# FF2 of a two-block transformer in fp32: activation sums, weight splits and outputs in another order, the norm row copied to SBUF, a longer held product

## Chip, cores and metric

One core of a Trainium2 chip. The metric is the device time of one execution in microseconds; lower is better.

## The reference

Two transformer blocks run one after the other on x of 1024 tokens by 1024 columns, in float32. The part that matters here is the feed-forward end of the second block:

```python
h = rmsnorm(x, pre_ffn_w[l])
f = (jax.nn.silu(h @ w_gate[l]) * (h @ w_up[l])) @ w_down[l]
x = x + rmsnorm(f, post_ffn_w[l])
```

`w_gate` and `w_up` are 1024 by 2816, `w_down` is 2816 by 1024. Everything before it (attention, convolution, pooling, the first feed-forward part, differential and neighbourhood attention) is computed by the same program ahead of this part, and no edit touches it.

## The kernel before, in words

**Precision.** Every fp32 product is made of three fp32r matmuls, high x high, high x low, low x high. A weight or an activation is split in two steps: ACT copies `raw` to fp32r (the high half), DVE subtracts it from `raw` (the low half). So a weight goes SP (load), ACT (high), DVE (low), TensorE. Activations lie transposed: features on 128 partitions, tokens along the free dimension, in two halves of 512 tokens (`HALF`).

**Engines.** There is no scheduler. For each engine a method writes its instructions in order (`pe_ff2`, `act_ff2`, `dve_ff2`, `pool_ff2`, `sp_ff2`), and semaphores join them. An engine works strictly down its list: a wait holds all that stands behind it. SP issues all DMAs of this part.

**The start of FF2 (in the trace from about 2174 us).** The 22 feature tiles of gate and up are each `g` and `u`. The first three (`PLAIN`) are plain products. `pe_ff2` runs g1's second half with the norm's statistics `stats7` inside it, u1 with the norm's rows `rows7` inside, then g2 and u2. On DVE: `gate_half` and `gate_whole` multiply the gate product by the norm row (RB), `gated` multiplies `up` by the Silu, `norm_recip` is the reciprocal of the norm, `w_low` makes a weight's low half. On ACT: `w_high` makes the high half, `up` and `up_whole` copy the up product to UU (`up_whole` waits until the spill of an earlier tile has read it), `silu`, `norm_sqrt`, the copy of the norm row to RB.

**Strassen.** The other 19 tiles (`NQ`) run by Strassen's scheme in seven parts a tile (`part`), each 12 matmuls of 512 columns. It needs sums of activation blocks: `second(k)` on ACT makes a scaled copy (`snap`), `sums(k)` on DVE makes four sums into `tr`, `sums_high(k)` on ACT and `sums_low(k)` on DVE split them into `th` and `tl`. Four k in all. SP's first weight loads of this stage (`gate_load(0)`, `up_load(0)`, into `swr`) wait for the last sums. The weights get sums (`s_sums`, on `swr`) and splits (`swh`, `swl`) of their own. The results of a tile go through `gate`, `shared`, `shared_end`, `gate_end`, `value`, `value_end` on DVE. `spill(i)` on SP writes each finished tile of 128 x 1024 (`uu`) to HBM (`scr_u`).

**The down product.** 88 slabs w = 22 p + k: token half p // 2, output half p % 2 (four output tiles n, each in a bank of its own), 22 slabs of features k. A slab is a weight tile of 128 x 512 (`dwr`, split into `dwt`; nine buffers, so that slab w's load waits for the end of slab w - 9) and an activation tile of 128 x 512 read back from `scr_u` (`DUR`, split into `DU`, in the trace `AH`, `AL` and `du`), and 12 matmuls of 512 columns. p = 0 and 2 use banks 0 to 3, p = 1 and 3 banks 4 to 7. `evacuate(p)` on DVE multiplies four finished banks by RB into YD. ACT squares them (`square`), POOL adds the squares (`accD`), TensorE turns these into the norm of the first token half: `stats(8, ...)` into bank 7, `rows(0, 6)` into bank 6. DVE then scales the eight output tiles of that half by the row in bank 6 (eight `scalar_tensor_tensor`, counted in `fmu`), and POOL adds x.

**The held part and the end.** Of the last p only the first `HELD` slabs are run over 512 tokens; ACT copies these partial sums to YD. The remaining 22 - `HELD` slabs are run for 256 tokens and then for the other 256, so that the final norm can begin with the first 256. The loop over w waits for all 88 slabs' low halves before these two groups. `out(g, n)` on DVE adds the partial sum and multiplies by RB.

**The turn.** In the last Strassen tile (n = 18) DVE makes seven weight splits and four activation splits between `gate_end` and `value`.

The wait of TensorE at slab 66 (`pe_ff2`), and the splits ahead of `value` at the turn (`dve_ff2`):

```python
            if w == 66:
                q.wait_ge(S.fmu, 8)
...
                for w in range(7):
                    d_low(w)
                    if w < 4:
                        u_low(w)
            value(n)
```

In the trace all matmuls have line 225, DVE's `tensor_tensor` line 193, its `scalar_tensor_tensor` line 196, ACT's activations line 190, DMA issues line 232.

## Time and profile before

| | |
|---|---|
| median of 3 runs | 2907.8 us (2907.36 to 2908.87) |
| the profiled execution | 2905.17 us, span 2902.9 us |
| TensorE busy | 2820.1 us (97%), 12895 matmuls |
| DVE, ACT, POOL busy | 1563.9 us (54%), 1032.5 us (36%), 369.5 us (13%) |
| mean granted TensorE clock | 0.99 |

The profiled execution's own time is 2.3 us above its span. TensorE's busy share says that it is the bound almost everywhere; it does not say where it stands. For that the waits of one engine are read (who ended each idle time, how long), then the table of stretches: how many matmuls were issued in a stretch, and the clock that was granted there.

### The profile page before, as it was taken

The numbers are of one execution on the slowest core, as the hardware profiler recorded it, in microseconds if no ns is written. First come the engines' busy times: TensorE is split into PE (matmuls) and PEld (weight loads), VectorE is DVE, ScalarE is ACT, GpSimd is POOL, SyncE is SP. The second block draws the span as 40 slices with busy tenths as digits, with TensorE's granted clock in tenths as the row PEclk, the third lists the DMA queues.
The fourth block names the chain that finished last, engine by engine and source line by source line (L and its number), as shares of the span: only waits on it lengthen the run. The fifth ranks groups of instructions, "written<-read, shape, count | busy, mean of one in ns | idle before, by whom it ended". The sixth has DMA issues, their size and how long they took to land.

```text
span 2902.9 us, 31767 instructions
## 1 busy us (share of the span) xinstructions
PE 2820.1 (97%) x12895; PEld 2286.5 (79%) x12895; DVE 1563.9 (54%) x1948; ACT 1032.5 (36%) x1396; POOL 369.5 (13%) x326
## 2 busy tenths in 40 slices
PE   9999999999999999999999999999999999999987
PEld 7877668888888888788878888666787788887876
DVE  7776544453545454543324444665647777764533
ACT  4313442331212121331235665655354322223422
POOL 1213112000000000111002222123421000000120
PEclk9999999999999999999999999999999999999998
DMA  3224523111111111144623322665641322225632
GB/s 118 88 73 141 151 61 111 51 40 55 46 53 41 58 35 61 56 148 151 218 80 100 99 78 77 196 199 150 222 160 59 102 80 87 87 86 172 199 116 95
DMA packets 105041, 304.62 MB, mean 105 GB/s; under 512 B 14392, under 2 KB 19128, under 8 KB 104896
## 3 DMA queue, kind: packets, MB, share of 16 engines
q1 hardware_dynamic: 90400, 256.22, 28.4%
q0 software_dynamic: 14496, 46.38, 4.6%
q8 instruction: 102, 1.67, 0.2%
q14 instruction: 43, 0.35, 0.0%
HBM read 238.42 MB, written 64.13 MB: 104 GB/s over the span
## 4 chain that ended last, share of the span: by engine, by line
PE 83%; DVE 8%; ACT 4%; issue 2%; DMA 2%; POOL 1%; SPq 0%; DVEq 0%; POOLq 0%; ACTq 0%
PE ps L225 82%; DVE cacc L196 2%; ACT PB L190 1%; PE ps L228 1%; POOL ga L193 1%; DVE PB L196 1%; DMA RBc<-scr_inv 1%; DVE AL L196 0%; DVE YA L193 0%; DVE dwt L193 0%; ACT gt L190 0%; ACT AH L190 0%; DVE stk L193 0%; DVE tr L196 0%; ACT stk L190 0%
## 5 line engine op out<-in xcount | busy, mean ns | idle before, releaser
L225 PE MATMUL ps<-AH,wh 128*128 128x512 f32 (+1 forms) x1608 | 644.7, 401 | 27.3 <-DVE wl L193 9.2
L225 PE MATMUL ps<-AH,wl 128*128 128x512 f32 (+1 forms) x1608 | 629.4, 391 | 0.0
L225 PE MATMUL ps<-AL,wh 128*128 128x512 f32 (+1 forms) x1608 | 629.0, 391 | 0.0
L193 DVE TENSOR_TENSOR wl<-raw,wh 128x1024 fp32r<-128x1024 f32 (+2 forms) x154 | 196.3, 1275 | 405.0 <-ACT wh L190 404.8
L225 PEld LDWEIGHTS ps<-AH,wh 128*128 128x128 f32 (+1 forms) x1608 | 302.1, 188 | 103.3 <-issue 18.8
L225 PEld LDWEIGHTS ps<-AH,wl 128*128 128x128 f32 (+1 forms) x1608 | 301.8, 188 | 66.8
L225 PEld LDWEIGHTS ps<-AL,wh 128*128 128x128 f32 (+1 forms) x1608 | 302.5, 188 | 64.3 <-issue 2.9
L190 ACT ACTIVATE wh<-raw 128x1024 fp32r<-128x1024 f32 (+4 forms) x201 | 188.1, 936 | 370.5 <-PE ps L225 367.8
L225 PE MATMUL ps<-stk,stk 128*128 128x512 f32 (+3 forms) x832 | 242.3, 405 | 12.2 <-DVE small L205 6.3
L225 PEld LDWEIGHTS ps<-stk,stk 128*128 128x128 f32 x832 | 146.6, 190 | 80.7 <-issue 32.4
L225 PE MATMUL ps<-UH,wh 128*128 128x512 f32 x528 | 205.5, 389 | 0.0
L225 PE MATMUL ps<-UH,wl 128*128 128x512 f32 x528 | 205.4, 389 | 0.0
L225 PE MATMUL ps<-UL,wh 128*128 128x512 f32 x528 | 205.4, 389 | 0.0
L225 PE MATMUL ps<-AH,dwt 128*128 128x512 f32 (+1 forms) x528 | 165.5, 392 | 16.0 <-DVE yd L196 7.7
L193 POOL TENSOR_TENSOR wl<-raw,wh 128x1024 fp32r<-128x1024 f32 (+3 forms) x47 | 102.3, 2176 | 321.2 <-ACT wh L190 321.1
L196 DVE SCALAR_TENSOR_TENSOR cv<-ub,vec,cv 128x1024 f32<-128x1024 f32 x88 | 113.1, 1285 | 54.7 <-ACT cv L190 53.1
L225 PEld LDWEIGHTS ps<-AH,dwt 128*128 128x128 f32 x528 | 101.3, 193 | 37.2 <-issue 8.1
L193 DVE TENSOR_TENSOR dwt<-dwr,dwt 128x512 fp32r<-128x512 f32 x88 | 66.2, 767 | 105.7 <-ACT dwt L190 105.5
L225 PE MATMUL ps<-th,swh 128*128 128x512 f32 x304 | 118.3, 389 | 0.0
L225 PE MATMUL ps<-tl,swh 128*128 128x512 f32 x304 | 118.3, 389 | 0.0
L225 PE MATMUL ps<-th,swl 128*128 128x512 f32 x304 | 118.3, 389 | 0.0
L225 PEld LDWEIGHTS ps<-UH,wl 128*128 128x128 f32 x528 | 99.1, 188 | 20.7
(267 smaller groups left out, 4701.1 us busy)
## 6 DMA issues: line engine op xcount, KB each, us to landing
raw<-in_w_up SPq DMA_DIRECT2D x44, 512.0 KB, 3.3
dwr<-in_dn SPq DMA_DIRECT2D x88, 256.0 KB, 2.9
swr<-in_w_gu SPq DMA_DIRECT2D x38, 512.0 KB, 3.7
raw<-in_w_w2in SPq DMA_DIRECT2D x32, 512.0 KB, 4.3
scr_u<-uu SPq DMA_DIRECT2D x22, 512.0 KB, 5.1
xin<-in_xT SPq DMA_DIRECT2D x16, 512.0 KB, 8.7
stk<-scr_ka SPq DMA_DIRECT2D x32, 256.0 KB, 8.1
raw<-in_w_w2v SPq DMA_DIRECT2D x16, 512.0 KB, 3.3
```

The source lines that it names most:

```text
L190: return Issued(self, self.e.activation(out, in_, func, **kw))
L193: return Issued(self, self.e.tensor_tensor(out, a, b, op))
L196: return Issued(self, self.e.scalar_tensor_tensor(out=out, in0=a, scalar=s, in1=b, op0=op0, op1=op1))
L225: return Issued(self, self.e.matmul(out, l, r, start=start, stop=stop))
L228: return Issued(self, self.e.transpose(out, a, ident))
```

## The change

Six edits, all in FF2:

- Start: DVE makes activation sums 0 before u1's low half, sums 1 and 2 before the second gate half, g2's low half before sums 3. ACT makes g2's high half before the first Silu and takes the splits of the sums earlier. u2's low half on DVE now stands behind `sums_low(3)`.
- SP issues `spill(0)` behind the first Strassen loads.
- Turn: each output step of the last Strassen tile comes ahead of a pair of splits. SP loads the activation slabs in step with the weight slabs, and may do so from the part on that last reads the memory they go to.
- Outputs `evacuate(p)` and their squares are spread over four slabs each, one tile a slab, instead of four at once; statistics go from slab 52 to 53.
- The norm row of the first half is copied by ACT from bank 6 to a new SBUF tile RD (semaphore `nrb`); DVE's eight products read RD, and TensorE waits at slab 66 for the copy instead of for the products.
- HELD 14 -> 17, so 5 slabs instead of 8 are left for the two 256-token groups; ACT's copies of the held part come after its last weight split.

```diff
--- before.py
+++ after.py
@@ -21,7 +21,7 @@
 PLAIN = 3
 NQ = NFF - PLAIN
 DW = 9
-HELD = 14
+HELD = 17
 BASE = 16512
 TOP = 229344
 
@@ -438,6 +438,7 @@
             self.DU.append(tuple(w.get("du", [P, 512], F32R)[:, :] for _ in range(2)))
         self.YD = w.get("yd", [P, NT, NTOK])
         self.accD = w.get("accd", [P, 512])
+        self.RD = w.get("rd", [P, 512])
         assert w.at <= lo + 76 * 1024
         self.sqD = [Area(nc, lo + at * 1024, lo + at * 1024 + 2048).get("sqd", [P, 512]) for at in (4, 6)]
         self.XD = Area(nc, lo + 80 * 1024, lo + 112 * 1024).get("xd", [P, NT, NTOK])
@@ -3047,8 +3048,8 @@
             if k == 0:
                 q.wait_ge(S.fe, 4 * (p - 1))
             if w == 66:
-                q.wait_ge(S.fmu, 8)
-            if w == 52:
+                q.wait_ge(S.nrb, 8)
+            if w == 53:
                 q.wait_ge(S.fe, 8)
                 q.wait_ge(S.aD, 7)
                 stats(8, 0, 4, 7)
@@ -3138,25 +3139,24 @@
             q.wait_ge(sem, v)
             q.act(self.DU[u % 22][0], self.DUR[u % 22], ACT.Copy).then_inc(S.duh)
 
-        for k in range(2):
+        for k in range(3):
             second(k)
         self.w_high(q, TILE["gu", ("u", 1)])
-        second(2)
         up(TILE["gu", ("u", 0)], 0)
+        sums_high(0)
+        second(3)
         self.norm_sqrt(q, 7, 4, 4)
+        sums_high(1)
         q.wait_ge(S.nrow, 7)
         q.act(self.RB[:, HALF[1]], self.bank(5), ACT.Copy).then_inc(S.nrb)
         up(TILE["gu", ("u", 0)], 1)
-        sums_high(0)
-        second(3)
+        self.w_high(q, TILE["gu", ("g", 2)])
         silu(0)
-        sums_high(1)
-        self.w_high(q, TILE["gu", ("g", 2)])
         sums_high(2)
+        sums_high(3)
         up_whole(1)
         silu(1)
         self.w_high(q, TILE["gu", ("u", 2)])
-        sums_high(3)
         for b in (0, 5, 4, 2):
             high(0, b)
         up_whole(2)
@@ -3193,16 +3193,17 @@
             if 30 <= w < 52:
                 u_high(w - 8)
             for p in range(3):
-                if w == 22 * (p + 1) + 4:
-                    for n in range(4):
-                        square(p // 2, 4 * (p % 2) + n)
-            if w == 60:
+                if 0 <= w - 22 * (p + 1) - 8 < 4:
+                    square(p // 2, 4 * (p % 2) + w - 22 * (p + 1) - 8)
+            if w == 61:
                 self.norm_sqrt(q, 8, 4)
-            if w == 66 + HELD + 1:
-                for n in range(4):
-                    q.wait_ge(S.dn, 12 + n + 1)
-                    q.wait_ge(S.fe, 12)
-                    q.act(self.YD[:, 4 + n, HALF[1]], self.d_bank(3, n), ACT.Copy).then_inc(S.fe)
+            if w == 66:
+                q.wait_ge(S.nrow, 8)
+                q.act(self.RD[:, :], self.bank(6), ACT.Copy).then_inc(S.nrb)
+        for n in range(4):
+            q.wait_ge(S.dn, 12 + n + 1)
+            q.wait_ge(S.fe, 12)
+            q.act(self.YD[:, 4 + n, HALF[1]], self.d_bank(3, n), ACT.Copy).then_inc(S.fe)
         c = slice(768, 1024)
         for n in range(4):
             q.act(self.YD[:, n, c], self.YD[:, n, c], ACT.Copy, scale=self.V("postff", n)).then_inc(S.fy)
@@ -3289,23 +3290,23 @@
             q.wait_ge(S.duh, u + 1)
             q.tt(l, self.DUR[u % 22], f32(h), ALU.subtract).then_inc(S.dul)
 
+        sums(0)
         self.w_low(q, TILE["gu", ("u", 1)])
         gate_half(0)
+        sums(1)
         self.norm_recip(q, 7, self.rc8[:, 4:8], 4)
+        sums(2)
         gate_half(1)
-        sums(0)
-        sums(1)
+        sums_low(0)
+        self.w_low(q, TILE["gu", ("g", 2)])
+        sums(3)
+        sums_low(1)
         gated(0)
-        self.w_low(q, TILE["gu", ("g", 2)])
-        sums_low(0)
-        sums_low(1)
-        sums(2)
+        sums_low(2)
         gate_whole(1)
         gated(1)
+        sums_low(3)
         self.w_low(q, TILE["gu", ("u", 2)])
-        sums_low(2)
-        sums(3)
-        sums_low(3)
         s_sums(0)
         s_lows(0, 0, 1, 2, 3)
         gate_whole(2)
@@ -3359,25 +3360,38 @@
             shared(n)
             if more:
                 s_lows(n + 1, 0)
+            else:
+                d_low(0)
+                u_low(0)
             shared_end(n)
             if more:
                 s_lows(n + 1, 1, 2)
+            else:
+                d_low(1)
+                u_low(1)
             gate_end(n)
             if more:
                 s_lows(n + 1, 3)
             else:
-                for w in range(7):
-                    d_low(w)
-                    if w < 4:
-                        u_low(w)
+                d_low(2)
+                u_low(2)
             value(n)
+        d_low(3)
         value_end(NQ - 1)
-
-        def evacuate(p):
+        u_low(3)
+        for w in range(4, 7):
+            d_low(w)
+
+        def evacuate(p, n):
             c = HALF[p // 2]
-            for n in range(4):
-                q.wait_ge(S.dn, 4 * p + n + 1)
-                q.tt(self.YD[:, 4 * (p % 2) + n, c], self.d_bank(p, n), self.RB[:, c], ALU.mult).then_inc(S.fe)
+            q.wait_ge(S.dn, 4 * p + n + 1)
+            q.tt(self.YD[:, 4 * (p % 2) + n, c], self.d_bank(p, n), self.RB[:, c], ALU.mult).then_inc(S.fe)
+
+        def normed(n):
+            c = HALF[0]
+            q.wait_ge(S.nrb, 8)
+            q.wait_ge(S.sD, 8)
+            q.stt(self.YD[:, n, c], self.YD[:, n, c], self.V("postff", n), self.RD[:, :], ALU.mult, ALU.mult).then_inc(S.fmu)
 
         for w in range(88):
             if w >= 7:
@@ -3387,16 +3401,13 @@
             if 30 <= w < 52:
                 u_low(w - 8)
             for p in range(3):
-                if w == 22 * (p + 1) + 2:
-                    evacuate(p)
-            if w == 60:
+                if 0 <= w - 22 * (p + 1) - 7 < 4:
+                    evacuate(p, w - 22 * (p + 1) - 7)
+            if w == 61:
                 self.norm_recip(q, 8, self.last_col(0), 4)
             if 67 <= w < 71:
-                q.wait_ge(S.nrow, 8)
-                for n in (2 * (w - 67), 2 * (w - 67) + 1):
-                    q.wait_ge(S.sD, 8)
-                    q.stt(self.YD[:, n, HALF[0]], self.YD[:, n, HALF[0]], self.V("postff", n), self.bank(6), ALU.mult,
-                          ALU.mult).then_inc(S.fmu)
+                normed(2 * w - 134)
+                normed(2 * w - 133)
 
         def out(g, n):
             at = slice(256 * (g - 1), 256 * g)
@@ -3512,12 +3523,13 @@
                 self.d_done(q, 22 + k)
             elif k < 4:
                 q.wait_ge(S.gem, GEM_END[TILE["gu", ("u", 2)]])
+            elif k < 16:
+                q.wait_ge(S.prd, 7 * (NQ - 1) + (1 if k < 8 else 2 if k % 2 == 0 else 5))
             else:
                 q.wait_ge(S.prd, 7 * NQ)
             q.dma(self.DUR[k], self.io["s_u"][k, :, HALF[t]]).then_inc(sem, 16)
 
         self.w_load(q, TILE["gu", ("u", 2)])
-        spill(0)
         q.wait_ge(S.tr3, 16)
         for i in (2, 3):
             at, base = self.x3_sem(i)
@@ -3529,6 +3541,7 @@
         q.wait_ge(S.xs, 24)
         gate_load(0)
         up_load(0)
+        spill(0)
         spill(1)
         q.wait_ge(S.gem, GEM_END[TILE["gu", ("u", 2)]])
         gate_load(1)
@@ -3544,11 +3557,12 @@
             if n == NQ - 1:
                 for w in range(7):
                     d_load(w)
-                    if w < 4:
-                        u_load(w)
-                for u in range(4, 8):
-                    u_load(u)
+                    u_load(w)
+        u_load(7)
+        u_load(8)
         spill(PLAIN + NQ - 1)
+        u_load(9)
+        u_load(10)
 
         def store(g, n):
             c = (HALF[0], slice(512, 768))[g]
@@ -3557,7 +3571,7 @@
 
         for w in range(7, 88):
             d_load(w)
-            if w < 21:
+            if 10 <= w < 21:
                 u_load(w + 1)
             if 29 <= w < 51:
                 u_load(w - 7)
```

How the order of instructions moves, at three places on DVE.

**DVE, start of FF2.** `wl` is a weight's low half (the first is u1's, the last g2's), `tr` the activation sums (four instructions a group), `gg` a gate product, `small` the norm's reciprocal, `tl` the low half of a group of sums, `uu` the finished slab. Before:

```order
L193 TENSOR_TENSOR wl_58<-raw_56,wh_57 128x1024 [waits s_wh]
L193 TENSOR_TENSOR gg_191<-ps,RB_59 128x512 [waits s_nrb,s_gem]
L216 RECIPROCAL small_53<-small_53 128x4 [waits s_nsq]
L193 TENSOR_TENSOR gg_191<-ps,RB_59 128x512 [waits s_nrb,s_gem]
L196 SCALAR_TENSOR_TENSOR tr_201<-YA_181,vec_49,snap_188 128x512 [waits s_gh,s_x3a]
L196 SCALAR_TENSOR_TENSOR tr_201<-YA_181,vec_49,snap_188 128x512
L196 SCALAR_TENSOR_TENSOR tr_201<-YA_181,vec_49,tr_201 128x512 [waits s_po] x2
L196 SCALAR_TENSOR_TENSOR tr_202<-YA_181,vec_49,snap_189 128x512 [waits s_gh,s_x3a]
L196 SCALAR_TENSOR_TENSOR tr_202<-YA_181,vec_49,snap_189 128x512
L196 SCALAR_TENSOR_TENSOR tr_202<-YA_181,vec_49,tr_202 128x512 [waits s_po] x2
L193 TENSOR_TENSOR uu_192<-uu_192,gg_191 128x1024 [waits s_fu,s_ex]
L193 TENSOR_TENSOR wl_58<-raw_56,wh_57 128x1024 [waits s_wh]
```

With the change (the four instructions of sums 0, `tr_201`, stand right ahead of the first row):

```order
L193 TENSOR_TENSOR wl_58<-raw_56,wh_57 128x1024 [waits s_wh]
L193 TENSOR_TENSOR gg_191<-ps,RB_59 128x512 [waits s_nrb,s_gem]
L196 SCALAR_TENSOR_TENSOR tr_202<-YA_181,vec_49,snap_189 128x512 [waits s_gh,s_x3a]
L196 SCALAR_TENSOR_TENSOR tr_202<-YA_181,vec_49,snap_189 128x512
L196 SCALAR_TENSOR_TENSOR tr_202<-YA_181,vec_49,tr_202 128x512 [waits s_po] x2
L216 RECIPROCAL small_53<-small_53 128x4 [waits s_nsq]
L196 SCALAR_TENSOR_TENSOR tr_203<-YA_181,vec_49,snap_190 128x512 [waits s_gh,s_x3a]
L196 SCALAR_TENSOR_TENSOR tr_203<-YA_181,vec_49,snap_190 128x512
L196 SCALAR_TENSOR_TENSOR tr_203<-YA_181,vec_49,tr_203 128x512 [waits s_po] x2
L193 TENSOR_TENSOR gg_191<-ps,RB_59 128x512 [waits s_nrb,s_gem]
L193 TENSOR_TENSOR tl_197<-tr_201,th_193 128x2048 [waits s_fga]
L193 TENSOR_TENSOR wl_58<-raw_56,wh_57 128x1024 [waits s_wh]
```

Sums 1 and 2 (`tr_202`, `tr_203`) have moved ahead of the second gate product, and the second `wl` stands behind the first `tl` and ahead of the product into `uu`.

**DVE, the turn.** `dwt<-dwr` is the low half of a weight slab, `AL<-alr` that of an activation slab, `snap`, `gg` and `uu` the outputs of the last Strassen tile. Before, the end of the splits and the outputs behind them:

```order
L193 TENSOR_TENSOR dwt_257<-dwr_255,dwt_256 128x512 [waits s_tyc]
L193 TENSOR_TENSOR dwt_260<-dwr_258,dwt_259 128x512 [waits s_tyc]
L193 TENSOR_TENSOR dwt_263<-dwr_261,dwt_262 128x512 [waits s_tyc]
L193 TENSOR_TENSOR uu_192<-ps,snap_190 128x512 [waits s_qmr,s_tr]
L193 TENSOR_TENSOR uu_192<-ps,snap_189 128x512
L193 TENSOR_TENSOR uu_192<-ps,uu_192 128x512 [waits s_bev,s_tr]
L193 TENSOR_TENSOR uu_192<-uu_192,gg_191 128x1024 [waits s_ex,s_bev]
L193 TENSOR_TENSOR AL_55<-alr_219,AH_54 128x512 [waits s_wac] x3
```

With the change:

```order
L193 TENSOR_TENSOR snap_190<-snap_189,ps 128x512 [waits s_bev,s_tr]
L193 TENSOR_TENSOR dwt_249<-dwr_247,dwt_248 128x512 [waits s_tyc]
L193 TENSOR_TENSOR AL_55<-alr_219,AH_54 128x512 [waits s_wac]
L193 TENSOR_TENSOR gg_191<-snap_190,ps 128x512 [waits s_vt,s_tr]
L193 TENSOR_TENSOR gg_191<-gg_191,RB_59 128x1024 [waits s_bev]
L193 TENSOR_TENSOR dwt_252<-dwr_250,dwt_251 128x512 [waits s_tyc]
L193 TENSOR_TENSOR AL_55<-alr_219,AH_54 128x512 [waits s_wac]
L193 TENSOR_TENSOR uu_192<-ps,snap_190 128x512 [waits s_qmr,s_tr]
L193 TENSOR_TENSOR uu_192<-ps,snap_189 128x512
L193 TENSOR_TENSOR dwt_255<-dwr_253,dwt_254 128x512 [waits s_tyc]
L193 TENSOR_TENSOR uu_192<-ps,uu_192 128x512 [waits s_bev,s_tr]
L193 TENSOR_TENSOR uu_192<-uu_192,gg_191 128x1024 [waits s_ex,s_bev]
```

The outputs now stand between the splits, with at most two splits ahead of one.

**DVE, from slab 67 on.** `yd<-ps,RB` is `evacuate` of p = 2, the `scalar_tensor_tensor` rows are the eight products with the norm row. Before:

```order
L196 SCALAR_TENSOR_TENSOR yd_238<-yd_238,vec_49,ps 128x512 [waits s_qsq,s_nrow]
L196 SCALAR_TENSOR_TENSOR yd_238<-yd_238,vec_49,ps 128x512
L193 TENSOR_TENSOR dwt_260<-dwr_258,dwt_259 128x512 [waits s_tyc]
L193 TENSOR_TENSOR yd_238<-ps,RB_59 128x512 [waits s_tsc] x4
L196 SCALAR_TENSOR_TENSOR yd_238<-yd_238,vec_49,ps 128x512 x2
L193 TENSOR_TENSOR dwt_263<-dwr_261,dwt_262 128x512 [waits s_tyc]
L196 SCALAR_TENSOR_TENSOR yd_238<-yd_238,vec_49,ps 128x512 x2
L193 TENSOR_TENSOR dwt_266<-dwr_264,dwt_265 128x512 [waits s_tyc]
L196 SCALAR_TENSOR_TENSOR yd_238<-yd_238,vec_49,ps 128x512 x2
```

With the change:

```order
L196 SCALAR_TENSOR_TENSOR yd_238<-yd_238,vec_49,rd_240 128x512 [waits s_qsq,s_nrb]
L196 SCALAR_TENSOR_TENSOR yd_238<-yd_238,vec_49,rd_240 128x512
L193 TENSOR_TENSOR dwt_261<-dwr_259,dwt_260 128x512 [waits s_tyc]
L196 SCALAR_TENSOR_TENSOR yd_238<-yd_238,vec_49,rd_240 128x512 x2
L193 TENSOR_TENSOR dwt_264<-dwr_262,dwt_263 128x512 [waits s_tyc]
L196 SCALAR_TENSOR_TENSOR yd_238<-yd_238,vec_49,rd_240 128x512 x2
L193 TENSOR_TENSOR dwt_267<-dwr_265,dwt_266 128x512 [waits s_tyc]
L196 SCALAR_TENSOR_TENSOR yd_238<-yd_238,vec_49,rd_240 128x512 x2
L193 TENSOR_TENSOR dwt_270<-dwr_268,dwt_269 128x512 [waits s_tyc]
L193 TENSOR_TENSOR dwt_246<-dwr_244,dwt_245 128x512 [waits s_tyc]
L193 TENSOR_TENSOR dwt_249<-dwr_247,dwt_248 128x512 [waits s_tyc]
L193 TENSOR_TENSOR yd_238<-ps,RB_59 128x512 [waits s_tsc]
```

The products read `rd` and wait for `nrb`, and the four `evacuate` instructions of p = 2 no longer stand among them.

## Rows read from the trace of the kernel before

**Rows 1.** Waits of TensorE from 2200 us on: us in total, times, longest us.

```profile
PE ps L225 <- DVE yd L196: 7.7, 1, 7.7
PE ps L225 <- DVE dwt L193: 5.1, 1, 5.1
PE ps L225 <- DVE swl L193: 4.1, 1, 4.1
PE ps L225 <- DVE wl L193: 3.9, 1, 3.9
PE ps L225 <- DVE uu L193: 3.2, 1, 3.2
```

**Rows 2.** Stretches: length; busy us (count) of PE, PEld, DVE, ACT, POOL; clock; DMA; GB/s.

```profile
2226.00:2240.00 14.00, 10.13 (x34) 7.88 (x33) 10.82 (x9) 5.41 (x5) 0.00 (x0) 0.76 0.10 39
2254.00:2268.00 14.00, 9.90 (x37) 7.67 (x36) 10.77 (x13) 6.03 (x8) 0.00 (x0) 0.88 0.44 156
2268.00:2622.00 354.00, 354.00 (x1564) 293.21 (x1562) 249.95 (x314) 99.58 (x119) 0.00 (x0) 1.00 0.27 85
2624.00:2638.00 14.00, 10.83 (x41) 8.48 (x41) 8.38 (x13) 4.10 (x7) 0.00 (x0) 0.88 0.68 217
2808.00:2828.00 20.00, 12.30 (x42) 9.62 (x41) 12.91 (x16) 5.05 (x10) 12.64 (x9) 0.74 0.15 46
```

**Rows 3.** Timeline at the start: start, us, engine, operation, count, [idle before <-releaser]; spill landings.

```profile
2217.49 0.69 DVE L193 TENSOR_TENSOR gg<-ps,RB 128x512 f32<-128x512 f32 x1 [4.00 <-ACT RB L190]
2218.10 1.41 DVE L196 SCALAR_TENSOR_TENSOR tr<-YA,vec,snap 128x512 f32<-128x512 f32 x2
...
2228.79 1.22 DVE L193 TENSOR_TENSOR wl<-raw,wh 128x1024 fp32r<-128x1024 f32 x1 [1.52 <-ACT wh L190]
...
2239.17 1.00 ACT L190 ACTIVATE uu<-ps 128x1024 f32<-128x1024 f32 x1
...
2241.16 1.23 DVE L193 TENSOR_TENSOR uu<-uu,gg 128x1024 f32<-128x1024 f32 x1 [2.71 <-ACT gg L190]
...
2254.75 2.75 DVE L193 TENSOR_TENSOR swr<-swr 128x512 f32<-128x512 f32 x4 [1.86 <-DMA swr<-in_w_gu]
...
DMA to landing us min/median/max: 2.6/4.5/6.5
```

**Rows 4.** Timeline of DVE at the turn.

```profile
2623.89 1.89 DVE L193 TENSOR_TENSOR dwt<-dwr,dwt 128x512 fp32r<-128x512 f32 x3
2625.70 1.28 DVE L193 TENSOR_TENSOR uu<-ps,snap 128x512 f32<-128x512 f32 x2
```

**Rows 5.** Timeline round slab 66, DVE and POOL; issue and landing of weight slabs (page).

```profile
2807.07 2.73 DVE L193 TENSOR_TENSOR yd<-ps,RB 128x512 f32<-128x512 f32 x4 [10.38 <-PE ps L225]
2809.71 1.40 DVE L196 SCALAR_TENSOR_TENSOR yd<-yd,vec,ps 128x512 f32<-128x512 f32 x2
2811.03 1.38 DVE L193 TENSOR_TENSOR dwt<-dwr,dwt 128x512 fp32r<-128x512 f32 x1
...
2810.59 8.30 POOL L193 TENSOR_TENSOR yd<-yd,xd 128x512 f32<-128x512 f32 x6 [12.76 <-DVE yd L196]
...
dwr<-in_dn SPq DMA_DIRECT2D x88, 256.0 KB, 2.9
```

**Rows 6.** Timeline at the end of the held part and in the tail.

```profile
2863.12 0.55 PE L225 MATMUL ps<-AH,dwt 128*128 128x256 f32 x1 [5.14 <-DVE dwt L193]
...
2868.61 2.32 PE L225 MATMUL ps<-du,dwt 128*128 128x256 f32 x18
2870.77 0.28 PE L225 MATMUL ps<-AH,dwt 128*128 128x256 f32 x1
...
2855.98 2.64 ACT L190 ACTIVATE yd<-ps 128x512 f32<-128x512 f32 x4 [13.82 <-PE ps L225]
2858.51 3.22 ACT L190 ACTIVATE dwt<-dwr 128x512 fp32r<-128x512 f32 x6
...
2889.12 0.42 DVE L193 TENSOR_TENSOR yd<-ps,yd 128x256 f32<-128x256 f32 x1 [0.53 <-PE ps L225]
```

## The prediction

> **What bounds the kernel now.** The profile's first part, in the table above, has TensorE busy for 2820.1 of a 2902.9 us span, so only time in which it stands, or runs at its lower clock, can be won. I read the stretch that the change touches, 2200 us to the end, through TensorE's own waits [rows 1]: five stalls of 3.2 to 7.7 us, every one ended by a DVE instruction. Then the table by stretch [rows 2] tells what a stall costs with the slow run behind it: in 2268 to 2622 us TensorE issues 1564 matmuls in 354 us without a pause at a granted clock of 1.00, so 0.226 us each. In the same number of microseconds round a stall there are fewer. 2226 to 2240: 34 where 61.9 fit, 27.9 x 0.226 = **6.3 us** lost, for an idle time of 3.9. 2254 to 2268: 37, **5.6 us** for 4.1. 2624 to 2638: 41, **4.7 us** for 3.2. 2808 to 2828: 42 where 88.4 fit, **10.5 us** for 7.7. The mean granted clock there is 0.74 to 0.88: after such a pause TensorE runs some microseconds at 1.2 instead of 2.4 GHz, and these come back with the stall. The fifth, 5.1 us at 2863, is followed by 30 matmuls of 256 columns in 5.49 us (2863.12 to 2868.61), where 18 take 2.16 us (2868.61 to 2870.77), 0.12 each: 5.1 + 1.9, with the rest of the last matmul's slot **7.2 us** [rows 6]. All five: 34.3 us.
>
> **The start (first two stalls, 11.9 us).** TensorE wants the low half of weight g2 at 2226.2 (it comes 3.9 us later, with DVE's `wl` of 2228.79). DVE had waited 1.52 us for ACT's high half, which stood behind a Silu and a split of activation sums, both late because DVE makes the sums only after the norm row [rows 3]. In the new order DVE makes sums 0, 1 and 2 before that, in its own waits for the norm: 4.00 us idle before 2217.49 [rows 3] and two shorter ones. A group of sums is two pairs at 1.41 us, 2.9 us; three are 8.7, so that they just fit and the gate half ends at 2218.1 as before (the square root's reciprocal comes 0.8 us later than before, at 2214.1, and TensorE asks for it at 2215.7). ACT takes g2's high half right after its second copy of `up`, near 2217.9. Behind the gate half DVE has sums-low 0 (2.3, twice a 128x1024 split) and g2's low half (1.14 to the next start), ready at **2221.5**, so 4.7 us early. The first stall goes. Sums 3 end at 2224.4 (2.9 more), 24 us earlier, and the first Strassen loads, which wait for them, land near 2229 and not at 2254.75, where DVE's first `swr` waited 1.86 us for them [rows 3]. The second stall goes too: TensorE would reach that unit near 2249, and the first low half of it is ready near 2242.
>
> **What comes in its place.** The spill of slab 0 now stands on SP behind the four sums and two 512 KB loads. Those are issued by 2225.5, and the spill itself waits for `gated(0)`, which by the sums above (2224.4, sums-low 1 2.3, product 1.14) ends at 2227.8. ACT's copy `up_whole(1)` waits for its landing, and behind that in a row are, by the starts of rows 3: copy and Silu 2.0, product 1.1, and on DVE now also sums-low 3 (2.3) ahead of u2's low half (1.2). The two landings here took 2.6 and 6.5 us [rows 3]; with two loads in flight I take 3.5, nearer the undisturbed one. So u2's low half is ready at 2227.9 + 3.5 + 6.6 = 2238.0, and TensorE wants it 48 matmuls after 2226.2, at 2237.0: a new stall of **1.0 us**. Bounds: 2.6 gives 0.2, 6.5 gives 4.0 and with it a slow stretch as in rows 2, 6.3 in all.
>
> **The turn (third stall, 4.7 us).** DVE splits seven weight slabs and four activation slabs ahead of the last unit's outputs: the last three weight splits are at 2623.89, the `uu` outputs only at 2625.70 [rows 4], and TensorE's fourth bank waits for them. Now at most two pairs stand ahead of any output. The last product of that unit ends near 2622.5, where the third stretch of rows 2 ends; the output add takes 0.7 us from there, and TensorE wants the bank nine matmuls later, at 2624.5. Nothing is left of the stall. Slabs 4 to 6 and their activations are split by 2629, wanted from 2633. SP: loads of slabs 5 and 6 now stand behind activation loads that wait for ACT, 2 to 3 us later than before, with 15 us to spare. Loads 7 and 8 wait for the last spill, issued near 2624.6 where it was 2629; they land near 2633 and are wanted at 2641. Price nothing; without that cover it would be up to 3 us.
>
> **Slab 66 (fourth stall, 10.5 us).** TensorE waits there for all eight scaled outputs, because they read the norm row in bank 6, which slab 66 overwrites. On DVE six of the eight stand behind the four outputs of the slabs before (2807.07), which end with slab 65 itself [rows 5]. Now TensorE waits only for ACT's one copy of the row (0.6 us, by the copies of 128x512 in rows 6) to SBUF. ACT comes to it when slab 66's weights have landed: released by slab 57's end, 2.9 us of landing [rows 5] and a 0.63 us split, so slab 59 or so; the row itself is written ahead of slab 58. Seven slabs of 2.7 us to spare, so nothing is left. The statistics go from slab 52 to 53 and wait for squares that ACT and POOL finish near slab 48. Outputs spread one per slab take 0.69 us of the 2 us that DVE idles in each.
>
> Here a rule speaks against the change. Of DVE and POOL together the trace shows: while POOL adds (2810.59, six in 8.30 us), a DVE split with two SBUF inputs takes 1.38 us, where three of them take 1.89 elsewhere [rows 4], and a pair of the products with a PSUM input keeps 1.40 us [rows 5]. The eight products now read the row from SBUF, and may become 1.38 us too: 8 x 0.7 = 5.6 us more DVE work over four slabs. DVE is ready 8 slabs ahead less 4.3 us of landing and splits, 17 us, so I cost it at nothing. The Trainium skill, page "SBUF — State Buffer", section "Who interferes with whom", says that the port pair of VectorE and GpSimd is an exclusive lock, taken by a VectorE operation with two SBUF inputs against a GpSimd one that reads SBUF; by it the copy to SBUF makes these products wait. The 1.38 us agree; the sum by it would be a lower gain only if the 17 us were not there.
>
> **The end of the held product (fifth stall, 7.2 us), and the tail.** ACT copies four banks when the held part ends (2855.98), and only then makes the last six high halves (2858.51, 3.22 us) [rows 6]; TensorE waits for all 88 low halves. Now the copies stand behind all splits, and the last slot's load is released four slabs (10.9 us) before the held part ends, for 4.3 us of latency. The stall goes. The held part is three slabs longer: 36 matmuls of 512 columns for 72 of 256: 8.15 against 8.64 us, 0.5 won. But the last group of a tile is now 15 matmuls (1.8 us) instead of 24 (2.88), and DVE's last output waited 0.53 us for TensorE [rows 6]; it comes 0.55 us late now, and the reciprocal of the second norm some 0.2 us late. Sum of this part -0.3, bounds -2 and +1.
>
> **Sum:** 6.3 + 5.6 + 4.7 + 10.5 + 7.2 - 1.0 - 0.3 = **33.0 us**. The profiled execution took 2905.2 us (span 2902.9), so 2872.2; the median of its runs lies 2.6 us above that execution, so I forecast **2874.8 us**, 1.1% faster. A measurement tells about 0.2% (5.8 us) from no change.
>
> **Rivals.**
> 1. *The start wins only half* (0.10). The spill's landing takes the 6.5 us that its second instance took; u2's low half comes 4 us late with a slow stretch: 5.3 us less, 2880.1. For it: two loads in flight. Against: they are issued 3 us before it.
> 2. *The turn keeps its stall* (0.06). If the activation slabs arrive late, DVE stands in `u_low(0)` or `u_low(1)` ahead of the outputs: 4.7 us less, 2879.5. Against: DVE's splits there ran without a wait [rows 4], and the waits of the outputs between them are longer than one pair of splits.
> 3. *The lock reaches TensorE* (0.04): by the rule above, the doubled products and splits during POOL's adds hold up a low half: 5.6 us less, 2880.4.
> 4. *No change* (0.02): each freed stall comes back at the next wait, as it would if DMA or DVE were the bound behind TensorE. In 2268 to 2622 DVE is busy 250 of 354 us and DMA 27% [rows 2], so hardly.
> 5. *Slower* (0.05): the granted clock. With the stalls gone TensorE runs from about 2238 to 2888 without a pause; if a stretch of such length made the clock fall to 1.2 GHz, each matmul would cost 0.226 us more. From 172 matmuls on (14 slabs) the 33 us and 5.8 more are eaten. Over 24 of the 88 slabs it would be 65 - 33 = 32 us slower, 2907.8 + 32 = 2940. Against: 354 us at 1.00 [rows 2]. No row shows 650.
>
> The forecast itself has 0.73, with a range of its own of 2870 to 2880 by the bounds above. Faster by over 0.2%: 0.73 + 0.10 + 0.06 + 0.04 = 0.93; within 0.2%: 0.02; slower: 0.05. The range takes in rivals 1 to 3 and a profile that is 2 us off: 2869 to 2885.
>
> **What would show it.** TensorE's waits after 2200 us should hold no `wl`, `swl`, `uu`, `yd` or `dwt` entry above 1.5 us, except one of about 1 us at u2's low half near 2237. Slab 66 should follow slab 65 without a gap. The granted clock should be 1.00 throughout. DVE's products from the copied row should take about 0.7 us, or 1.4 beside POOL. The last output add should start 0.8 us after TensorE's last 256-column matmul (0.2 before). A stall over 3 us at u2, at the turn or at a held boundary would prove the step of that part wrong; a clock under 0.95 in any 15 us after 2240 would prove rival 5.

## The result, and the profile after

| | before | changed |
|---|---|---|
| median | 2908.34 us of 4 runs (2907.36 to 2909.48) | 2876.61 us of 4 runs (2873.5 to 2879.08) |
| ratio, 95% interval | | 0.989 [0.9873, 0.9907] |
| the profiled execution | 2905.17 us, span 2902.9 | 2877.44 us, span 2875.2 |
| first wait of this part | 2202.74 us | 2208.62 us |
| from there to the span's end | 700.2 us | **666.6 us** |

1.1% faster. The forecast was 2874.8 us for the median and 2872.2 for the profiled execution. This one came 5.2 us later than that, and the fourth row of the table says where: it *entered* the changed part 5.9 us later than the execution before did, after 2200 us of the same instructions. From the entry on, 33.6 us are gained, where the sum of the prediction said 33.0; by the medians it is 31.7. So I compare kernels below by this **entry-to-end time** (span less the start of TensorE's first matmul behind `AL`), and by medians beside it.

TensorE's waits from 2200 us on, in the changed kernel; all five of [rows 1] are gone, and the `wl` of 1.7 us is the new one at u2's low half:

```profile
PE ps L225 <- DVE accd L193: 3.1, 1, 3.1
PE ps L225 <- DVE AL L196: 1.9, 2, 1.2
PE ps L225 <- DVE wl L193: 1.7, 1, 1.7
PE ps L225 <- DVE small L216: 1.0, 1, 1.0
```

The table by stretch, with the columns of [rows 2]: round the turn, round slab 66, and all from u2's low half to the last matmuls.

```profile
2612.00:2626.00 14.00, 14.00 (x63) 11.59 (x62) 11.05 (x16) 4.26 (x7) 0.00 (x0) 1.00 0.60 196
2790.00:2810.00 20.00, 20.00 (x90) 16.54 (x89) 15.95 (x16) 6.22 (x11) 11.52 (x8) 1.00 0.31 95
...
2246.00:2860.00 614.00, 614.00 (x2776) 511.06 (x2775) 375.23 (x499) 193.78 (x281) 26.57 (x18) 1.00 0.36 115
```

Slab 66 stands in the second: 90 matmuls in 20 us without a pause, where [rows 2] had 42. The third row is 614 us at a granted clock of 1.00, TensorE's level of 2.4 GHz, which rival 5 called in question.

The timeline of the start, which answers to [rows 3]; subtract 5.9 us to compare it with the times in the prediction:

```profile
2226.19 1.22 DVE L193 TENSOR_TENSOR wl<-raw,wh 128x1024 fp32r<-128x1024 f32 x1
2230.34 0.80 SPq L232 DMA_DIRECT2D swr<-in_w_gu  x2
2233.68 7.93 SPq L232 DMA_DIRECT2D scr_u<-uu  x2
2238.02 1.03 ACT L190 ACTIVATE uu<-ps 128x1024 f32<-128x1024 f32 x1 [5.75 <-DMA scr_u<-uu]
2241.17 2.29 DVE L193 TENSOR_TENSOR tl<-tr,th 128x2048 fp32r<-128x2048 f32 x1
2243.37 1.22 DVE L193 TENSOR_TENSOR wl<-raw,wh 128x1024 fp32r<-128x1024 f32 x1
```

g2's low half starts at 2220.3 by the clock of the execution before, and ends where the prediction had it (2221.5). The spill of slab 0 is issued at 2233.68, and ACT's copy, which waits for its landing, starts at 2238.02: 4.3 us, where I had taken 3.5. Behind it stands the row that I had counted as necessary, sums-low 3, and then u2's low half; TensorE waits 1.68 us for it.

The end of the held part and the tail, which answer to [rows 6]:

```profile
2843.26 2.64 ACT L190 ACTIVATE yd<-ps 128x512 f32<-128x512 f32 x4 [5.24 <-PE ps L225]
...
2858.70 2.03 PE L225 MATMUL ps<-du,dwt 128*128 128x256 f32 x15
2861.04 0.42 DVE L193 TENSOR_TENSOR yd<-ps,yd 128x256 f32<-128x256 f32 x1
2863.86 0.60 PE L225 MATMUL ps<-cst,accd 128*128 128x1 f32 x4 [3.13 <-DVE accd L193]
```

ACT waits for TensorE there, and no longer the reverse. The last matmuls start near 2860.3, and the last output add stands at 2861.04, 0.7 us behind.

### The profile page after: what moved, and what is told of

Same layout as the page of the kernel before. It is cut to its first block, busy times and chain, and to the rows that moved or that the text cites. A ratio compares the mean times of both kernels' runs of the same rounds, so it can differ in the third digit from the quotient of the medians.

```text
span 2875.2 us, 31699 instructions
## 1 busy us (share of the span) xinstructions
PE 2813.0 (98%) x12859; PEld 2280.6 (79%) x12859; DVE 1565.4 (54%) x1948; ACT 1033.0 (36%) x1397; POOL 370.1 (13%) x326
## 4 chain that ended last, share of the span: by engine, by line
PE 84%; DVE 8%; ACT 3%; issue 2%; DMA 1%; POOL 1%; SPq 0%; DVEq 0%; POOLq 0%; ACTq 0%
PE ps L225 83%; DVE cacc L196 2%; ACT PB L190 1%; PE ps L228 1%; POOL ga L193 1%; DVE PB L196 1%; DMA raw<-in_w_win 0%; DVE YA L193 0%; DVE AL L196 0%; DMA RBc<-scr_inv 0%; DVE stk L193 0%; DVE sqacc L193 0%; ACT gt L190 0%; ACT AH L190 0%; DVE wl L193 0%
## 5 line engine op out<-in xcount | busy, mean ns | idle before, releaser
L225 PE MATMUL ps<-stk,stk 128*128 128x512 f32 (+3 forms) x832 | 245.5, 410 | 11.1 <-DVE small L205 5.2
L225 PE MATMUL ps<-AH,dwt 128*128 128x512 f32 x512 | 158.9, 389 | 0.0
L225 PEld LDWEIGHTS ps<-UH,wh 128*128 128x128 f32 x528 | 99.1, 188 | 20.6
```

The costliest lines, as they stand in the source:

```text
L225: return Issued(self, self.e.matmul(out, l, r, start=start, stop=stop))
```

## The experiments

Twelve runs. The first five put one or two parts of the change alone on the kernel before, to see whether the parts add and whether each cause is the one named; the others go out from the changed kernel.

### The start alone

VectorE's, ScalarE's and SyncE's rows of the start as in the change, of which a few lines:

```diff
+        sums(0)
         self.w_low(q, TILE["gu", ("u", 1)])
         gate_half(0)
+        sums(1)
...
         up_load(0)
+        spill(0)
         spill(1)
```

> Only the edits of the start (sums and splits re-ordered on VectorE and ScalarE, spill of slab 0 behind the first two Strassen loads), on the kernel before; the other stalls stay. Theory (parts add): the two stalls of 6.3 and 5.6 us go, a stall of 1.7 us at u2's low half comes, so 10.2 us less between the first wait of this part and its end, median near 2898; the stalls dwt 5.1, yd 7.7 and uu 3.2 us stay in TensorE's waits within 0.3 us. Rival (a freed stall moves to the next wait): less than 7 us gained, and one of these three grows. Second question, the 5.9 us by which the changed kernel's profiled execution entered this part late: if systematic (something in the changed kernel's set-up), the entry near 2202.7 here says that the start edits are not its cause; if it is spread between executions, entries will scatter over 2202 to 2209 in all kernels of this study.

Measured: 2898.94 us, ratio 0.9965 [0.9953, 0.9977]; entry 2209.55, entry-to-end 688.7 us, **11.5 less** than before. The two stalls are gone, `wl` 1.4 is there, `yd` 7.7, `dwt` 5.1 and `uu` 3.2 stayed as they were. The theory of parts that add holds here, with 1.3 us more than it said. Part of that is not the edit's: the slow stretches behind the three stalls that stayed came out 0.4 us shorter in all than in the profile of before (the last section shows how far they differ). From the entry to the start of the turn's wait, where only this edit acts, the time falls from 421.9 to 410.8 us, by 11.1. The entry was as late as 2209.55, and the kernel up to there is that of before.

### The turn alone

```diff
             shared(n)
             if more:
                 s_lows(n + 1, 0)
+            else:
+                d_low(0)
+                u_low(0)
...
+            elif k < 16:
+                q.wait_ge(S.prd, 7 * (NQ - 1) + (1 if k < 8 else 2 if k % 2 == 0 else 5))
```

> Only the edits of the turn (outputs of the last Strassen unit between the weight splits, activation loads released earlier), on the kernel before. Theory (parts add): the stall of 3.2 us at the fourth bank goes with its slow stretch, 4.7 us less, median near 2903.6; swl 4.1, wl 3.9, yd 7.7, dwt 5.1 us stay. Rival (turn needs the earlier start): the stall stays or moves, under 2 us gained.

Measured: 2903.45 us, 0.9983 [0.9974, 0.9992]; entry-to-end 694.9 us, **5.3 less**. TensorE has no wait at all from 2600 to 2650 us. As predicted, within 0.6.

### The copied row alone

```diff
             if w == 66:
-                q.wait_ge(S.fmu, 8)
+                q.wait_ge(S.nrb, 8)
...
+            if w == 66:
+                q.wait_ge(S.nrow, 8)
+                q.act(self.RD[:, :], self.bank(6), ACT.Copy).then_inc(S.nrb)
```

> Only the copy of the norm row to SBUF, with TensorE's wait at slab 66 put on that copy, on the kernel before; outputs of each quarter still in one block of four. Theory (the wait on the row's readers is the whole stall): the 7.7 us wait and its slow stretch go, 10.5 us less, median near 2897.8. VectorE's products from the copied row take 1.4 us where they run beside GpSimd's adds and 0.7 without. Rival (VectorE's backlog is the cause, and spreading the outputs is what cures it): a wait for a low half or for yd of over 2 us is left near slab 66 to 72, and less than 7 us is gained.

Measured: 2902.03 us, 0.9976 [0.9968, 0.9985]; entry-to-end 693.8 us, only **6.4 less** of 10.5 (a part of what is missing has nothing to do with the edit, see the next run). Slab 66 follows slab 65 without a gap, but five slabs on TensorE waits for a low half, that of slab 71. The timeline of that kernel (engines as named in each row; waits in brackets):

```profile
2816.64 1.31 ACT L190 ACTIVATE sqd<-yd 128x512 f32<-128x512 f32 x2
2826.89 2.90 POOL L193 TENSOR_TENSOR yd<-yd,xd 128x512 f32<-128x512 f32 x2 [0.69 <-DVE yd L196]
2829.75 4.39 POOL L193 TENSOR_TENSOR accd<-accd,sqd 128x512 f32<-128x512 f32 x3
2831.12 0.63 ACT L190 ACTIVATE sqd<-yd 128x512 f32<-128x512 f32 x1 [13.17 <-POOL accd L193]
2831.66 4.79 ACT L190 ACTIVATE dwt<-dwr 128x512 fp32r<-128x512 f32 x9
2832.30 4.20 DVE L193 TENSOR_TENSOR dwt<-dwr,dwt 128x512 fp32r<-128x512 f32 x5 [4.90 <-ACT dwt L190]
2833.05 0.50 PE L225 MATMUL ps<-AH,dwt 128*128 128x512 f32 x1 [2.22 <-DVE dwt L193]
```

Read it from the bottom. TensorE waits for DVE, DVE for ACT's high halves, ACT had stood 13.17 us in its *fourth square*: that one needs the buffer of the second, which POOL frees by adding it up, and POOL's adds stand behind its totals, which follow DVE's products. The weight splits had piled up behind that square: nine run in a row after it. The rival's numbers came (a wait of over 2 us, less than 7 us gained), but not its cause: the stall comes over three engines, and the next run removes it with VectorE's outputs still in one block. In the kernel before, the same square waited 10.7 us for POOL as well:

```profile
2820.50 0.63 ACT L190 ACTIVATE sqd<-yd 128x512 f32<-128x512 f32 x1 [10.72 <-POOL accd L193]
```

That wait began under TensorE's stall of 7.7 us and outlasted it (the stall ended at 2816.77), but no wait of TensorE followed from it there.

### The copied row, and squares one slab apart

```diff
-                if w == 22 * (p + 1) + 4:
-                    for n in range(4):
-                        square(p // 2, 4 * (p % 2) + n)
+                if 0 <= w - 22 * (p + 1) - 8 < 4:
+                    square(p // 2, 4 * (p % 2) + w - 22 * (p + 1) - 8)
```

> The row copied to SBUF as in p_row, and ScalarE's four squares of each quarter one slab apart from the eighth slab on (the square root and the statistics one slab later), VectorE's outputs still in one block. Theory (the 2.2 us wait that p_row left comes from ScalarE, which stood 13.2 us in its fourth square for GpSimd's sum behind the six totals, with nine weight splits queued behind it): that wait goes, and the entry-to-end time falls from 693.8 to 700.2 - 10.5 = 689.7 us. Rival (VectorE's block of outputs and products is late by itself): a wait for dwt of over 1 us is left near slab 72, and the time stays above 692.

Measured: 2898.98 us, 0.9966 [0.9954, 0.9977]; entry-to-end 689.4 us, **10.7 less** than before and 4.3 less than with the copy alone. (ACT's root, DVE's reciprocal and the statistics stand one slab later too.) The wait is gone. But it was only 2.2 us long, and no slow stretch stood behind it, so 4.3 us can't all be the squares'. The wait at the turn and the one at the held part's end are in all three kernels, and the edits act between them. In order: the kernel before (its second row is in [rows 6]), the copy alone, the copy with the squares spread.

```profile
2627.83 0.50 PE L225 MATMUL ps<-AH,dwt 128*128 128x512 f32 x1 [3.17 <-DVE uu L193]
```

```profile
2635.97 0.50 PE L225 MATMUL ps<-AH,dwt 128*128 128x512 f32 x1 [3.18 <-DVE uu L193]
2863.08 0.55 PE L225 MATMUL ps<-AH,dwt 128*128 128x256 f32 x1 [5.23 <-DVE dwt L193]
```

```profile
2632.28 0.64 PE L225 MATMUL ps<-AH,dwt 128*128 128x512 f32 x1 [3.18 <-DVE uu L193]
2856.75 0.55 PE L225 MATMUL ps<-AH,dwt 128*128 128x256 f32 x1 [5.14 <-DVE dwt L193]
```

From the end of the first wait to the start of the second it is 230.2 us, 221.9 and 219.3. So the copied row is worth **8.3 us** and the spread squares **2.6**, together 10.8. Of the 4.3 us, the other 1.7 lie outside this stretch, most of it in longer slow stretches behind stalls that no edit of these two kernels touches. The fourth square still waits for POOL, but now late in the row of splits, so that few stand behind it:

```profile
2822.09 0.62 ACT L190 ACTIVATE sqd<-yd 128x512 f32<-128x512 f32 x1
2828.35 0.63 ACT L190 ACTIVATE sqd<-yd 128x512 f32<-128x512 f32 x1 [3.39 <-POOL accd L193]
```

### ScalarE's four bank copies alone

```diff
-            if w == 66 + HELD + 1:
-                for n in range(4):
-                    ...
+        for n in range(4):
+            ...
```

> Only ScalarE's four bank copies put behind the last six weight splits, with 14 slabs held as before, on the kernel before. Theory (the order on ScalarE is the whole stall): the 5.1 us wait at the held part's end and its slow stretch go, 7.2 us less, median near 2901.1. Rival (holding 17 slabs is needed too, since the last loads are released only one slab ahead): a wait of 1 us or more for dwt or wl is left at the end of the held part, and under 5 us is gained.

Measured: 2902.63 us, 0.9983 [0.9974, 0.9991]; entry-to-end 694.8 us, **5.4 less** of 7.2. The rival has the cause: a wait of 1.75 us is left (its "under 5 us gained" was too little). The timeline of that kernel:

```profile
2860.79 0.63 ACT L190 ACTIVATE dwt<-dwr 128x512 fp32r<-128x512 f32 x1 [2.22 <-DMA dwr<-in_dn]
2861.46 0.69 DVE L193 TENSOR_TENSOR dwt<-dwr,dwt 128x512 fp32r<-128x512 f32 x1 [2.16 <-ACT dwt L190]
2862.37 0.19 PEld L225 LDWEIGHTS ps<-AH,dwt 128*128 128x128 f32 x1 [2.15 <-DVE dwt L193]
2862.40 0.36 PE L225 MATMUL ps<-AH,dwt 128*128 128x256 f32 x1 [1.75 <-ACT yd L190]
```

The matmul's wait is put down to ACT's `yd`, but its weight load names the right one: the last slab's low half, whose load landed at 2860.79. It could only be issued when slab 78 was done, one slab ahead of the held part's end.

### The changed kernel with 14 slabs held

```diff
-HELD = 17
+HELD = 14
```

> The changed kernel with 14 slabs held instead of 17, so eight left for the two halves. Theory (the last load is released only one slab ahead of the held part's end, so that its low half is 1.7 us late): a wait of 1.7 us at the end of the held part, no slow stretch behind it, the last output add 0.2 and not 0.5 us behind TensorE's last 256-column matmul; 36 matmuls of 512 columns become 72 of 256, 0.5 us more. From the entry into this part to the end 666.6 + 1.7 + 0.5 - 0.6 = 668.2 us. Rival (the order of ScalarE's copies is all of the fifth stall, the number held is worth nothing): 666.6 us within 0.5 and no wait.

Measured: 2878.43 us, 0.9893 [0.9875, 0.9911]; entry-to-end 668.8 us. TensorE's waits: `yd` 1.7 at the held part's end, and 2.2 for `wl` at u2, 0.5 more than in the changed kernel. Without these 0.5, holding 17 is worth **1.7 us**, where the theory said 1.6. Together with the 5.4 above, 7.1 of 7.2.

### Three ways at u2's low half and the lock

The spill back ahead of the loads:

```diff
         self.w_load(q, TILE["gu", ("u", 2)])
+        spill(0)
         q.wait_ge(S.tr3, 16)
...
-        spill(0)
         spill(1)
```

> The changed kernel with the spill of slab 0 back ahead of the first Strassen loads. Theory (the 1.7 us wait at u2's low half is the spill's landing, 4.2 us beside two loads of 512 KB): alone the spill lands in 2.6 to 3.2 us, the wait shrinks to 0.1 to 0.7 us, the loads come 3.4 us later and nothing waits for them; entry-to-end 665.5 us. Rival A (a landing of this spill takes 4 us with or without loads): wait 1.7 us, 666.6 us. Rival B (the loads come too late then): a wait for swl appears near 2257 + 6 us, and it is no faster.

Measured: 2874.43 us, 0.9884 [0.9866, 0.9901]; entry-to-end 666.7 us, wait 1.7 us: nothing won, rival A's numbers, but not its cause. The rows:

```profile
2230.77 0.33 SPq L232 DMA_DIRECT2D scr_u<-uu  x1
2231.40 1.99 SPq L232 DMA_DIRECT2D swr<-in_w_gu  x2
2235.19 1.03 ACT L190 ACTIVATE uu<-ps 128x1024 f32<-128x1024 f32 x1 [5.83 <-DMA scr_u<-uu]
```

4.4 us from issue to ACT's start, as with the loads ahead. The loads are issued 0.6 us behind it, so it was not alone either. What it does alone stands in other traces: in the kernel before and in the four partial kernels without the edits of the start, the same spill is issued some 20 us ahead of the loads. Issues and landings (the last number, in us) of this one spill, in the kernel before and in the changed one:

```profile
scr_u<-uu SPq DMA_DIRECT2D x1, 512.0 KB, 2.6
```

```profile
scr_u<-uu SPq DMA_DIRECT2D x1, 512.0 KB, 4.3
```

Alone it lands in 2.6 us in all five profiles; with the two loads in flight, ahead of it or just behind it, in 4.0 to 5.0 in all nine. So it is the longer with the loads in flight, as the theory had it, and this edit did not part them from it. That loads issued 4.0 us later (counted from the entry) harm nothing is shown.

u2's low half ahead of the last sums' low half:

```diff
         gated(1)
-        sums_low(3)
         self.w_low(q, TILE["gu", ("u", 2)])
+        sums_low(3)
```

> The changed kernel with u2's low half ahead of the fourth sums' low half on VectorE. Theory: the low half is ready 2.3 us earlier, the 1.7 us wait goes, and the low half of the sums is wanted only by the fourth product of each part of the first Strassen unit, 11 us later; entry-to-end 664.9 us. Rival (the sums' low half or the first Strassen splits are then late by what was won): a wait for tl or swl of 1 us or more, entry-to-end 666 us or more.

Measured: 2871.45 us, 0.9872 [0.9855, 0.9889]; entry-to-end **664.8 us**, no `wl`, `tl` or `swl` wait. The theory, to 0.1.

GpSimd's totals behind all eight products:

```diff
         def total(g, n):
-            q.wait_ge(S.fmu, 8 * g + n + 1)
+            q.wait_ge(S.fmu, 8 if g == 0 else 8 + n + 1)
```

> The changed kernel with GpSimd's eight totals of the first half put behind all eight of VectorE's products from the copied row; the output is the same. Theory (a VectorE operation with two SBUF inputs and a GpSimd addition exclude each other by turns, so that both stretch, and TensorE is covered by seven slabs of lead): pairs of products 1.41 us in place of 2.44, the weight splits between them 0.69 in place of 1.78, GpSimd's eight totals 8 x 1.4 to 1.55 us, and no change of the entry-to-end time (666.6 within 0.5). Rival 1 (the products are slow by themselves, since they read the row from SBUF): 2.44 us still. Rival 2 (the late totals hold up the fourth square and with it weight splits, as in p_row): a wait for dwt of over 1 us near slab 80.

Measured: 2876.85 us, 0.989 [0.9876, 0.9905]; entry-to-end 667.4 us with a `wl` wait of 2.4 at u2, 0.7 more than in the changed kernel: 666.6 without it. No other wait. In the changed kernel, DVE and POOL near slab 66:

```profile
2783.88 1.41 DVE L196 SCALAR_TENSOR_TENSOR yd<-yd,vec,rd 128x512 f32<-128x512 f32 x2
2784.77 3.37 POOL L193 TENSOR_TENSOR yd<-yd,xd 128x512 f32<-128x512 f32 x2 [32.58 <-DVE yd L196]
2786.91 2.44 DVE L196 SCALAR_TENSOR_TENSOR yd<-yd,vec,rd 128x512 f32<-128x512 f32 x2
2789.28 1.77 DVE L193 TENSOR_TENSOR dwt<-dwr,dwt 128x512 fp32r<-128x512 f32 x1
```

and with the late totals:

```profile
2782.59 1.41 DVE L196 SCALAR_TENSOR_TENSOR yd<-yd,vec,rd 128x512 f32<-128x512 f32 x2
2784.67 0.69 DVE L193 TENSOR_TENSOR dwt<-dwr,dwt 128x512 fp32r<-128x512 f32 x1 [0.68 <-ACT dwt L190]
2789.66 11.85 POOL L193 TENSOR_TENSOR yd<-yd,xd 128x512 f32<-128x512 f32 x8 [42.30 <-DVE yd L196]
2795.58 1.81 DVE L193 TENSOR_TENSOR dwt<-dwr,dwt 128x512 fp32r<-128x512 f32 x1 [1.14 <-ACT dwt L190]
```

The same products take 1.41 us a pair without POOL and 2.44 beside it; a split 0.69 and 1.8. The pair of [rows 5] that read the row from PSUM met POOL's adds only at its end. The next one of that kernel lies wholly within them:

```profile
2812.33 1.39 DVE L196 SCALAR_TENSOR_TENSOR yd<-yd,vec,ps 128x512 f32<-128x512 f32 x2
```

It kept its 1.39 us. What stretches them is the two SBUF inputs beside POOL. The Trainium skill, page "SBUF — State Buffer", section "Who interferes with whom", calls this an exclusive lock between such a VectorE operation and a GpSimd one that reads SBUF. The rows agree: POOL's adds stretch too, 3.37 us a pair here and 2.90 in the kernel with the copied row alone, at 2826.89, where DVE was idle beside most of it. It costs TensorE nothing here.

### The changed kernel again, and two versions beyond it

> The changed kernel once more, unchanged, beside the kernel before. Theory (the 5.9 us by which the profiled execution of the changed kernel entered this part late is spread between executions): the entry falls anywhere in 2202 to 2210 us as in the ten profiles so far, and the time from there to the end of the span is 666.6 us within 0.8. Rival (the changed kernel enters late as a rule): entry at 2208 or later again, and the median of many runs 5 us above 2908.3 - 33.6 = 2874.7, that is near 2880.

Measured: 2874.35 us, 0.9882 [0.9865, 0.9898]; entry 2205.35, entry-to-end 667.0 us. The rival falls.

The tail re-ordered, on the kernel with u2's low half moved:

```diff
-        for n in range(4):
+        for n in range(3):
             scaled(n)
         out(2, 7)
         square(2, 6)
         square(2, 7)
-        for n in range(4, 8):
+        for n in range(3, 7):
             scaled(n)
         self.norm_recip(q, 10, self.last_col(2), 2)
+        scaled(7)
```

> The changed kernel with u2's low half ahead of the fourth sums' low half (as a_wlow), and in the tail three scaled outputs instead of four ahead of the last output, and the last scaled output behind the reciprocal. Theory: the last output add starts 0.1 to 0.2 us behind TensorE's last 256-column matmul instead of 0.5, one scaled output of 0.41 us leaves the path: entry-to-end 664.8 - 0.4 = 664.4 us, median near 2872. Rival (ScalarE's square or the norm's chain ends last there, not VectorE): 664.8 us.

Measured: 2873.22 us, 0.9879 [0.9864, 0.9893]; entry-to-end 665.1 us, nothing won at the span's end. From this kernel's timeline, and below it the last two rows of the kernel that only moves u2's low half:

```profile
2856.81 0.61 PE L225 MATMUL ps<-cst,accd 128*128 128x1 f32 x4 [2.45 <-DVE accd L193]
2861.98 2.42 DVE L193 TENSOR_TENSOR yd<-yd,xd 128x1024 f32<-128x1024 f32 x3
2854.41 10.79 SPq L232 DMA_DIRECT2D out<-yd  x11
```

```profile
2860.71 2.42 DVE L193 TENSOR_TENSOR yd<-yd,xd 128x1024 f32<-128x1024 f32 x3
2852.47 11.46 SPq L232 DMA_DIRECT2D out<-yd  x11
```

TensorE's wait for the statistics is 0.7 us shorter (2.45 for 3.13), and the gain reaches DVE's last adds: counted from the entry (2203.71 and 2202.07) they start at 658.3 us here and at 658.6 there, though a wait of 0.2 us at u2 holds this profile up. The last store takes it back. Its issue ends at 2865.2 and 2863.9, and the span ends 3.6 us behind it here and 3.0 us there. Over the 14 profiles that last piece lies between 3.0 and 3.6 us; whether the order in the tail has a part in it was not tried. So the rival's time came, but by these rows neither ScalarE nor the norm's chain stood in the way.

The same with 15 slabs held:

```diff
-HELD = 17
+HELD = 15
```

> comb with 15 slabs held and seven left for the two halves. Theory (one slab of lead, 2.7 us, more than covers the 1.7 us that a_held14 lacked): no wait at the held part's end; two slabs more in matmuls of 256 columns, 24 x 0.2267 = 5.44 against 48 x 0.12 = 5.76 us, 0.3 more; groups of 21 matmuls, 2.5 us, cover VectorE's work per output, 0.2 to 0.4 less; entry-to-end 664.4 us within 0.3. Rival (load latency varies by more than the slab): a wait of 1 us at the held part's end and over 665.5 us.

Measured: 2871.81 us, 0.9872 [0.9858, 0.9887]; entry-to-end 664.8 us, no wait at the held part's end. One slab of lead is enough. DVE's last adds start at 657.9 us from the entry, 0.75 before those of the kernel that only moves u2's low half, and again the last store takes 3.6 us and not 3.0. These two kernels are the best of the study, 1.8 us ahead of the changed kernel by entry-to-end time, too little for the medians to tell them from it.

## Why the prediction was right

| step | predicted us | measured us |
|---|---|---|
| start: two stalls go, one comes | 11.9 - 1.0 | 11.5 (11.1 up to the next wait), with a wait of 1.4 (1.7 to 2.4 in the changed kernel and its variants) |
| turn | 4.7 | 5.3 |
| slab 66 | 10.5 | 10.7 (10.8 between the neighbouring waits: 8.3 by the copied row, 2.6 by the squares) |
| held part's end and tail | 7.2 - 0.3 | 5.4 by the copies' order, 1.7 by holding 17 |
| sum | 33.0 | 34.6 added up, 33.6 in the changed kernel |

**What bounds it; parts that add.** Right: the time comes back stall by stall, with the slow run behind each, and in the full change no freed stall came back elsewhere. The parts add to within 1.0 us. Finer than that single profiles don't tell: the slow stretch behind one and the same stall cost up to 1.4 us more in one profile than in another. The prediction took its prices from the very profile against which the 33.6 us are counted, so these differences fall out of that comparison; by the medians, where they don't, it is 31.7 us. That the whole fits to 0.6 us is in part luck.

**The start.** The schedule held to a few tenths; the term that was mis-sized is the landing, 3.5 us taken, 4.1 to 5.1 found between the spill's issue and ACT's copy in nine profiles. I took a value nearer the undisturbed one, and the two loads made the landing longer than that. (Of the two landings in [rows 3], 2.6 us is this spill with nothing else in flight, 6.5 the next one behind two loads; the 4.5 is only their middle.) Hence a wait of 1.7 to 2.4 in the changed kernel and not 1.0. Rival 1 had the mechanism, but not the size: no landing of this spill took 6.5 us, and no slow stretch came. What I did not ask was whether sums-low 3 had to stand ahead of u2's low half at all: it did not.

**The turn.** Right; rival 2 fell.

**Slab 66.** The sum was right, the reason three quarters of it. "Seven slabs of 2.7 us to spare, so nothing is left", said of the copy, would have been 2.2 us short (8.3 of 10.5) without the spread squares. I had counted the spreading only as DVE work of 0.69 us a slab, and not asked what ACT's fourth square waits for. The spreading of DVE's outputs, the other half of that edit, was not needed for it: the 10.8 us came with the outputs still in one block.

**The lock.** Seen in kind as the prediction said, hidden; rival 3 fell. The sizes differ a little: products 0.7 or, beside POOL, about 1.2 each where it said 1.4, and a split 1.8 where it said 1.38.

**The end of the held part.** Both causes stand in the prediction, the copies' order and the load that is released too late; the copies' order made three quarters of it.

**The tail.** Holding 17 costs about what its wider matmuls win: with the wait of 1.7 us taken out, 14 and 17 slabs give the same time. The last output came 0.7 us behind TensorE's last matmul, as said.

**The clock.** 614 us at 1.00, so rival 5 fell. Rival 4 fell with the gain itself.

**The number.** The median came 1.8 us above the forecast (2876.6 for 2874.8), and when the same kernel was run again 0.45 below it. The 5.2 us between the forecast and the profiled execution lie ahead of the change. In 14 profiles of this study the entry falls between 2202.07 and 2209.94 us, both early and late for kernels of either kind; the profiled execution of before (2202.74) was an early one. The first wait for `AL`, behind the first weights, is part of it (1.0 us in an early profile, 3.5 in a late one); the rest was not traced.

## What to carry over

A wait that is taken away uncovers what queued in its shadow: ask, of each engine in the chain, for the longest wait that overlaps the old stall, also where it ends after it (here a 10.7 us wait of ACT for POOL beside a 7.7 us stall of TensorE). A step of a periodic loop that needs another engine is better spread one per turn than put in a block, since whatever is queued behind the block waits for its last member. And when an effect is 1% of a long program, compare the time from the entry into the changed part, not only the whole; and to say what one edit gave, compare the stretch between the waits next to it, which other stalls and their slow stretches don't reach.
